# The front's rounding in one pass with products released tile by tile, and all low parts of the gather stage on VectorE

## What is computed

```python
h = rms_norm(x, norm1_g) * (1 + scale1) + shift1          # modulate
proj = h @ w_in                                           # q, k, v, gates, ...
...
a = gelu(einsum('td,ted->te', h2, u_tab[experts]))        # 128 experts a token
w = gates * a
out = einsum('te,ted->td', w, v_tab[experts])
```

## Time and profile before

| | us |
|---|---|
| median of 3 runs | 2500.1 (2497.99 to 2506.24) |
| time of the profiled execution | 2501.1 |
| its span | 2499.4 |
| front | 0 to about 185 |
| mixers | to about 330 |
| `stage_first`, gathers from 437 on | to about 2044 |
| `stage_half` | to the end |

### The profile page before, as it was taken

How to read it: one execution, slowest core, us unless ns; L and a number is a source line. 1 busy time by engine, 2 the same in 40 slices (tenths; PEclk the granted TensorE clock), 3 DMA queues, 4 the chain that set the end, 5 groups by cost and what they waited for, 6 DMA issues and landing times. The chain is left out here.

```text
span 2499.4 us, 22306 instructions
## 1 busy us (share of the span) xinstructions
PE 2057.0 (82%) x7187; PEld 1278.5 (51%) x7187; DVE 1575.2 (63%) x2938; ACT 992.7 (40%) x2294; POOL 1251.8 (50%) x800
## 2 busy tenths in 40 slices
PE   5997867378999777777699888888999969687999
PEld 3785645244554232322356444445665647455787
DVE  4648546888886577765779875667887852452111
ACT  4215443133333222223453568445343334344443
POOL 3532000075765353444477444567898847004887
PEclk8986678689999899999899999899999989788999
DMA  7630035299999999999899999999999955003564
GB/s 263 232 121 1 1 133 152 93 419 406 420 420 405 421 421 421 422 421 421 350 358 377 409 404 344 377 378 380 419 418 407 418 208 155 26 1 93 171 191 153
DMA packets 128640, 726.60 MB, mean 291 GB/s; under 512 B 14471, under 2 KB 15498, under 8 KB 62986
## 3 DMA queue, kind: packets, MB, share of 16 engines
q0 software_dynamic: 74800, 540.59, 53.0%
q1 hardware_dynamic: 53088, 184.44, 21.2%
q10 hardware_dynamic: 634, 0.14, 0.0%
HBM read 716.45 MB, written 8.66 MB: 290 GB/s over the span
## 5 line engine op out<-in xcount | busy, mean ns | idle before, releaser
L1326 PE MATMUL ps<-uv_ring_a,expert_diag_a 128*128 128x512 f32 x1920 | 918.0, 624 | 232.9 <-ACT expert_diag_a L1308 214.6
L1107 POOL DMA_INDIRECT uv_ring_a<-in_peer_uv_dram,expert_idx x512 | 620.3, 1212 | 647.1 <-PE ps L1326 510.9
L1254 DVE CUSTOM_DVE_ANT_0 uv_ring_a<-uv_ring_a,x_rows 128x1024 f32<-128x1024 f32 x512 | 787.1, 1544 | 248.4 <-DMA uv_ring_a<-in_peer_uv_dram,expert_idx 246.8
L1326 PEld LDWEIGHTS ps<-uv_ring_a,expert_diag_a 128*128 128x128 f32 x1920 | 368.9, 198 | 699.9 <-issue 369.4
L1401 POOL TENSOR_TENSOR w_low_a<-w_raw_a,w_high_a 128x1024 fp32r<-128x1024 f32 x122 | 302.1, 2477 | 109.9 <-ACT w_high_a L1393 108.0
L1401 POOL TENSOR_TENSOR w_low_b<-w_raw_b,w_high_b 128x1024 fp32r<-128x1024 f32 x98 | 233.9, 2390 | 228.5 <-ACT w_high_b L1393 227.1
L1293 ACT ACTIVATE expert_gelu_a<-expert_dot_a 128x2 f32<-128x2 f32 x256 | 52.1, 204 | 691.0 <-DVE expert_dot_a L1254 690.7
L1393 ACT CAST w_high_a<-w_raw_a 128x1024 fp32r<-128x1024 f32 x146 | 152.0, 1042 | 192.5 <-PE ps L1414 172.5
L1308 ACT ACTIVATE expert_diag_a<-ident,expert_weight_a 128x128 f32<-128x128 f32 x480 | 168.5, 395 | 0.6 <-ACT expert_weight_a L1299 0.4
L1393 ACT CAST w_high_b<-w_raw_b 128x1024 fp32r<-128x1024 f32 x98 | 102.9, 1051 | 116.8 <-PE ps L1414 114.5
L1299 ACT ACTIVATE expert_weight_a<-expert_gelu_a,expert_gate 128x1 f32<-128x1 f32 x512 | 122.9, 286 | 8.6
(11 more groups left out here) (463 smaller groups left out, 3334.5 us busy)
## 6 DMA issues: line engine op xcount, KB each, us to landing
w_raw_a<-in_w_gu_dram SPq DMA_DIRECT2D x44, 512.0 KB, 7.8
w_raw_b<-in_w_gu_dram SPq DMA_DIRECT2D x44, 512.0 KB, 3.6
w_raw_a<-in_w_peer_q_dram SPq DMA_DIRECT2D x32, 512.0 KB, 7.1
w_raw_a<-in_w_out_dram SPq DMA_DIRECT2D x24, 512.0 KB, 7.7
w_raw_a<-in_w_in_dram SPq DMA_DIRECT2D x24, 512.0 KB, 6.2
w_raw_b<-in_w_in_dram SPq DMA_DIRECT2D x24, 512.0 KB, 3.8
w_raw_a<-in_w_down_dram SPq DMA_DIRECT2D x22, 512.0 KB, 7.8
w_raw_b<-in_w_down_dram SPq DMA_DIRECT2D x22, 512.0 KB, 3.6
```

Source lines behind the costliest of these rows:

```text
L1107: pool.indirect_dma_start(out=self.ring[:, n % self.RING, :], out_offset=None, in_=K.uv, in_offset=bass.IndirectOffsetOnAxis(ap=K.idx[self ...
L1254: dve.tensor_tensor_reduce(u, u, self.h[b][:, :], 1.0, 0.0, ALU.mult, ALU.add, self.a[:, s:s + 1]).then_inc(self.s_dot, 1)
L1326: ins = nc.tensor.matmul(self.bank(half), self.diag[q % self.DIAGS][:, :], self.ring[:, n % self.RING, D + 512 * half:D + 512 * half + 512 ...
```

## The change

In the front, ScalarE writes the high part directly from the modulation (`hi = round(hT * g1 + shift)`), with no instruction in between. VectorE, once `hi` k is there, makes the unrounded value in `hT` itself with a `tensor_scalar`, waits for it, and subtracts. TensorE's wait for the eight low parts is split: in the first product it waits for part k before the matmuls of k. In `stage_first`, GpSimd's stream of low parts is gone and VectorE's covers all 146 tiles; the places in the weave are the same. `stage_half` is unchanged.

```diff
-    def turned(self, pe, n, bank, x, cols=P):
+    def turned(self, pe, n, bank, x, cols=P, ready=None):
...
         pe.wait_ge(self.s_lo, n + 1)
         for k in range(KD):
+            if ready:
+                pe.wait_ge(ready, k + 1)
             last = split_product(self.K.nc, bank, (hi[:, k, 0:cols], lo[:, k, 0:cols]), x(k), k == 0, k == KD - 1)
...
             for k in range(KD):
                 act.wait_ge(s_xn, k + 1)
-                act.activation(K.hT[:, k, :], K.hT[:, k, :], ACT.Identity, scale=K.g1[:, k:k + 1],
-                               bias=shift[k]).then_inc(s_h, 1)
-                act.wait_ge(s_h, k + 1)
-                act.copy(hi[:, k, :], K.hT[:, k, :]).then_inc(s_hh, 1)
+                act.activation(hi[:, k, :], K.hT[:, k, :], ACT.Identity, scale=K.g1[:, k:k + 1],
+                               bias=shift[k]).then_inc(s_hh, 1)
...
             for n in range(VG):
-                if n == 0:
-                    pe.wait_ge(s_hl, KD)
-                else:
-                    if n >= 2:
-                        pe.wait_ge(*out(n - 2))
+                if n >= 2:
+                    pe.wait_ge(*out(n - 2))
...
-                    w.turned(pe, n, K.ps[n % 2][:, :], x)
+                    w.turned(pe, n, K.ps[n % 2][:, :], x, ready=None if n else s_hl)
...
             for k in range(KD):
                 dve.wait_ge(s_hh, k + 1)
+                dve.tensor_scalar(K.hT[:, k, :], K.hT[:, k, :], K.g1[:, k:k + 1], shift[k], ALU.mult, ALU.add).then_inc(s_h, 1)
+                dve.wait_ge(s_h, k + 1)
                 dve.tensor_tensor(lo[:, k, :], K.hT[:, k, :], hi[:, k, :].bitcast(F32), ALU.subtract).then_inc(s_hl, 1)
...
         @block.gpsimd
         def _(pool):
-            weave(rows_in(pool), g.pool(pool), W.lows(pool, dense))
+            weave(rows_in(pool), g.pool(pool))
...
         @block.vector
         def _(dve):
-            weave(g.dve(dve), W.lows(dve, 0, dense), bias.dve(dve), half.dve(dve, begin + 80.0), *(n.dve(dve, [(s_later, 16)]) for n in ahead),
+            weave(g.dve(dve), W.lows(dve), bias.dve(dve), half.dve(dve, begin + 80.0), *(n.dve(dve, [(s_later, 16)]) for n in ahead),
```

## The result

| | before | changed |
|---|---|---|
| median, first comparison | 2499.07 us (6 runs) | 2482.5 us (6 runs), ratio 0.9934 [0.9914, 0.9953] |
| median, second comparison, other chip job | 2498.41 us | 2480.12 us (6 runs), ratio 0.9933 [0.9912, 0.9955] |
| span of the profiled executions | 2499.4 us | 2470.1 and 2472.0 us |

The change saves 16.6 us, 0.7%; the brackets behind a ratio are its 95% interval. The profiled execution of the changed kernel (2471.84 us) is the fastest of its six, so the pair of spans shows 29.3 us where the medians show 16.6. The reading has to say which of the 29.3 belong to the change.

The account below looks back on a forecast made before the run. No engine was full overall: a serial ScalarE-VectorE chain bounded the front, DMA and TensorE stretches the gather stage. Span 2499.4 less 7.6 and 8 gave time 2485.5, or 2484.5 against the runs' median; range 2472 to 2491.

Parts of the forecast that it names:

- The front, 7.6 us forecast: Front: one rounding pass and TensorE starting behind the first low part end the first product 7.6 us earlier.
- The tight place at the `kTd` copy: Front: VectorE takes the first `kTd` copy 0.16 us after release; costed at no loss, but reason for the lower end.
- The gather stage, 8 us forecast: Gather stage: moving 122 low parts from GpSimd to VectorE shortens TensorE's waits, gaining 8 us.
- hardly: Stretches 500:800 and 1750:2000: DMA engines are full, so hardly any gain there reaches the end.
- 28.5 x 0.58 x 0.5: TensorE's waits in 1250:1400 and 1550:1750, times the lock's share, times half the blocking: 8 us gained.
- The new wait, costed at nothing: Gather stage: VectorE now waits for ScalarE's cast of each tile; covered by its idle time, so 0 us.
- idle until ACT w_high by tens of us: Sign of being wrong: VectorE standing idle tens of us for ScalarE's casts of weight tiles.
- VectorE's total: VectorE busy time: 149.3 us of low parts added, 160 us of interference removed; level or down by 10 us.
- Front only: Rival: DMA and TensorE hold the gather stage, so only the front's 7.6 us remain; 2492.5 us, chance 0.22.
- The lock as the brake of the stage: Rival: the VectorE-GpSimd port lock braked the gather stage, so 35 us come back there; 2457.5 us, chance 0.15.
- The starved issue: Rival: VectorE's extra work holds GpSimd's gather issues, costing about 14 us in the gather stage; 2506.5 us, chance 0.05.
- VectorE as the pace: Rival: low parts queue with dots on VectorE and delay gathers, 43 us lost after 1200; 2535.5 us, chance 0.10.

Follow-up runs that it names:

- front_wait8: Changed kernel, but TensorE again waits for all eight low parts before its first product; 2487.8 us, ratio 0.9953.
- after_again: The changed kernel itself, unmodified, run once more to see how far profiles differ; 2480.1 us, ratio 0.9933.
- lows_only: Changed kernel with the old front restored, including the single wait for eight low parts; all `stage_first` low parts on VectorE; 2489.0 us, ratio 0.9953.
- half_dve: Changed kernel with the 98 low parts of `stage_half` moved to VectorE too; 2478.7 us, ratio 0.9926.
- twice: Changed kernel with one more VectorE subtraction, into an unread tile, behind each of the 122 low parts taken over; 2568.3 us, ratio 1.0289.
- ghosts: Changed kernel with 122 unread GpSimd subtractions added at the places and behind the waits of its old low parts; 2609.9 us, ratio 1.0446.
- memsets: Changed kernel with two GpSimd memsets of 128x1024, reading nothing, at the place of each former GpSimd low part; 2483.4 us, ratio 0.9937.
- front_only: Changed kernel's new front, with GpSimd keeping the low parts of tiles 24 to 145 as before; 2487.6 us, ratio 0.996.
- own2: Changed kernel with VectorE adding every fourth v half from the third token block on, not the fourth only; 2487.1 us, ratio 0.9953.

## Why the prediction was right, and where it was not

The prediction had 2484.5 us, and the medians are 2482.5 and 2480.1. Faster was right. Of its two terms one is right in size and place, the other in size only.

**The front, 7.6 us forecast.** Front's end lies 7.6 us earlier in the means of the profiles (188.0 to 180.5); with profiles of one front 1.7 to 2.5 us apart, so close a match is luck. Its parts were off and cancelled. The multiply takes 0.54 us, not 0.4 (upper bound 0.75): I had halved the 0.75 of twice the columns, measured on a form with one scalar where this has two, and it did not halve; and the pitch is 1.185 us a tile, not 1.1: over seven tiles 0.6 us late. The first low part comes earlier than said, TensorE starts at 48.50 and not at 49.7: the lock held the first multiply to 47.63 and not to 48.9, since GpSimd's pair ran 1.2 us earlier (the stretch of the first old `h_low`, which I had read as 1.37 us, is 1.30), and `g1` was ready 1.2 us earlier as well (ScalarE starts at 45.10, not 46.30). That is chance: in the second profile of the same kernel ScalarE starts at 46.00 and TensorE at 49.41. The tight place at the `kTd` copy cost nothing that can be seen. What I did not say, and front_wait8 shows, is that nearly all of it, 6.4 of 7.6, is the split wait.

**The gather stage, 8 us forecast.** Five profiles with every low part on VectorE and nothing added (changed, after_again, front_wait8, lows_only, half_dve) have 1599.9 us in the mean, the two with GpSimd 1607.5: 7.6 us. The prices were right: 1.224 us a low part, 1.221 a dot. But the step that turned them into a gain put it in the wrong place. It took TensorE's waits in 1250:1400 and 1550:1750, 28.5 us, times two factors. These waits hardly shrank. Waits of the changed kernel in 1250:1400, then in 1550:1750:

```profile
POOL uv_ring_a L1106 <- PE ps L1325: 92.2, 42, 6.4
...
DVE w_low_a L1400 <- ACT w_high_a L1392: 22.1, 13, 4.6
...
PE ps L1325 <- ACT expert_diag_a L1307: 8.2, 7, 2.0
```

```profile
DVE w_low_a L1400 <- ACT w_high_a L1392: 43.6, 19, 6.1
...
PE ps L1325 <- ACT expert_diag_a L1307: 20.4, 6, 7.4
```

The diagonals have 8.2 us for 7.2 and 20.4 for 17.2, over the whole run 217.9 for 214.6; the wait for `ffn_low` went from 4.1 to 1.1. In windows moved with the work (1225:1375 and 1524:1724) the three sum to 25.5 us for 28.5, so 3.0 of the 8 are there at most. In the means over the same profiles block 1 became 5.9 us shorter and block 4 6.8, blocks 2 and 3 together 1.1 longer, and the end gave back 4.1. Blocks 1 and 4 hold the stretches 500:800 and 1750:2000, of which I had said that the DMA engines are full there and "hardly" any of it reaches the end. By the dots, the stretch from the 385th to the 433rd, nearly all of it in 1550:1750, from which the forecast took three quarters of its gain, even became 4.9 us longer.

That is the failed step, and with it the one before, that the lock was what held the stage. One missed row was GpSimd's longest wait for a cast: 59.84 us, at 441 to 501, ahead of my first stretch of the stage, with five gathers behind it. I had costed what stands behind the moved wait on VectorE and not what stood behind it on GpSimd, where it was taken away. Its price is less than its length, 3 to 4 us by gather or dot 33, since the changed kernel then waits 65.41 us for a place. In block 4 it was not waits: in 1750:2000 the GpSimd of the kernel before stood idle 1.8 us for casts, and was busy 222 of 250 us, with 2.4 us of subtraction for each tile ahead of its gathers.

The end, from the 512th gather on, is 4.1 us longer only by this mark: before, the last gather was issued 11.7 us late in the mean, but its dot began 6.0 late, and from the 512th dot on the kernels with every low part on VectorE are 1.6 us shorter. That 28.5 x 0.58 x 0.5 gave 8 is a coincidence.

**The new wait, costed at nothing.** VectorE waits 186 us for casts, 101 times. I had named "idle until ACT w_high by tens of us" as a sign of being wrong. It appeared, and the kernel was faster: the idleness took the place of idleness for gathers (53 us less) and of stretched instructions (165 us less in the dots alone). An idle time on an engine is a sign only with who stands behind it. But the place is dear. Between dots 385 and 433 of the changed kernel (1563.6:1734.9) the waits of VectorE have this row:

```profile
DVE w_low_a L1400 <- ACT w_high_a L1392: 41.1, 17, 6.1
```

VectorE is as busy there as before (115 and 117 us), GpSimd half as much, and the stretch is the one that became 4.9 us longer. So low parts on VectorE, wait and work together, cost about 5 us there net, where I had costed the wait at nothing. What the wait costs apart from the work is not measured: a kernel without it would need another source for the low parts.

**VectorE's total** was to stay level or fall by 10 us; it fell by 49. The lock had stretched others beside the dots: L1214 46.4 to 39.8 us, L1173 30.8 to 22.1, and a row of small ones.

**The rivals.** Front only (2492.5) lies outside both intervals, and the gather stage shortened in every such profile. The lock as the brake of the stage (2457.5) lies outside too: removing it whole gave 8 us and not 35. The starved issue did not come: the mean issue went from 1.212 to 1.148 us, the longest is 1.987, so a VectorE low part holds GpSimd's issue no longer than a dot did. VectorE as the pace did not come at this load, but twice puts its price at 0.64 us for each us added, which the rival had at 0.44 us a tile with the lock's share taken off. The lock costs some 125 us on top of the moved work (ghosts over memsets); taken away in exchange for that work it came out about even, within the spread of single profiles.

## What to carry to other kernels

Before a chain of tiles that a consumer waits for as a whole, split the wait first: here that alone gave 6.4 of 7.6 us, and the saved pass the rest. When work leaves an engine that issues DMAs, look at the longest waits of that work, at its own time and at the transfers queued behind both; the port lock may only pay for the move. Place the gain by marks that are the same work in both kernels, not by windows at fixed times, and take marks on the engine that uses the data beside those on the one that issues it: here a gather issued 12 us late was used 6 us late. An engine at 62% can still be at the edge: one experiment that doubles the moved work shows whether it is.

## What I had not expected: the mixers' time varies between like kernels

Between the front's last matmul and the end of the mixers the same instructions took 137.6 to 151.9 us in these profiles, in two groups and between them. The rows that move with it are the granted clock, the third number from the end (columns as in the earlier trace rows). Kernel before:

```profile
200.00:220.00 20.00, 14.62 (x78) 11.98 (x79) 18.13 (x33) 11.24 (x27) 7.08 (x4) 0.50 0.01 1
...
260.00:280.00 20.00, 16.90 (x89) 13.28 (x89) 12.27 (x20) 9.68 (x23) 0.00 (x0) 0.50 0.00 0
```

Changed kernel:

```profile
200.00:220.00 20.00, 16.02 (x128) 13.30 (x128) 17.71 (x35) 13.04 (x34) 3.90 (x2) 0.84 0.00 1
...
260.00:280.00 20.00, 16.13 (x130) 13.24 (x127) 12.81 (x29) 5.94 (x15) 0.00 (x0) 0.86 0.00 1
```

half_dve, whose front and mixers are the changed kernel's to the letter:

```profile
200.00:220.00 20.00, 19.94 (x102) 15.90 (x101) 14.67 (x28) 11.14 (x27) 2.69 (x2) 0.50 0.00 1
...
260.00:280.00 20.00, 17.33 (x96) 14.75 (x96) 12.78 (x19) 7.77 (x20) 0.00 (x0) 0.50 0.01 1
```

At 0.50 TensorE ran at 1.2 GHz for the whole stretch, at 0.84 to 0.86 mostly at 2.4 GHz; it is busy with short gaps either way (14.62 of 20 us, 16.02 of 20). The clock level there is not fixed by the change: the changed kernel's own second profile has 0.67 in 200:220 and takes 139.0 us, half_dve 148.0 with 0.50. Whether the change shifts the odds is not shown: the three profiles whose front ends late (before, lows_only, front_wait8) take 144.7 to 148.4, the eleven others 137.6 to 151.9. Why the one or the other comes is open. The Trainium skill, "TensorE: Matmul & The Clock Gate", section "Part 1: The HAM clock gate (the "warmup" mystery)", has the point at which the clock rises vary from run to run. These traces agree that it varies: the same 20 us have 0.84, 0.67 and 0.50.

Over all runs of this study a run's time falls by about 1.3 us for each 0.001 of its mean granted clock (my fit over 187 runs, with 3.2 us left over), so an odd 9 us in one profiled execution is within what chance gives. Brought to the same clock by that fit, memsets is 8.2 ± 2.3 us faster than before, the changed kernel 13.6 ± 2.7 and 15.0 ± 2.7 in the two comparisons, front_only 6.1 ± 2.0 and lows_only 9.9 ± 2.0: nearer to the 15.2 that front and gather stage give by their marks than the raw medians are. The fit has a limit. It would make own2 18.7 ± 2.1 us faster than before, and so faster than the changed kernel, against own2's median and its longer gather stage; between kernels that give TensorE different work it does not hold.
